# Previous value rows moved from SP's queue to ACT's in three pieces, and a deeper step pipeline in stick-breaking

## What is computed

```python
def stick_breaking(q, k, v, q_pos, k_pos):
    z = einsum('bqhd,bkhd->bhqk', q, k) * HEAD_DIM ** -0.5
    visible = k_pos[None, :] < q_pos[:, None]
    log_beta = log_sigmoid(z)
    log_keep = where(visible, log_sigmoid(-z), 0.0)
    later = cumsum(log_keep, axis=3, reverse=True) - log_keep
    w = where(visible, exp(log_beta + later), 0.0)
    return einsum('bhqk,bkhd->bqhd', w, v)
```

## Time and profile before

| | us |
|---|---|
| median of 3 runs | 1674.61 |
| lowest, highest | 1673.42, 1680.12 |
| the profiled execution, its own time | 1671.62 |
| its span, first to last instruction | 1670.0 |

### The profile page before, as it was taken

How to read it: one execution, slowest core, us unless ns; L and a number is a source line. 1 busy time by engine, 2 the same in 40 slices (tenths; PEclk the granted TensorE clock), 3 DMA queues, 4 the chain that set the end, 5 groups by cost and what they waited for, 6 DMA issues and landing times. The chain is left out here.

```text
span 1670.0 us, 31496 instructions
## 1 busy us (share of the span) xinstructions
PE 1452.1 (87%) x12700; PEld 1196.8 (72%) x12700; DVE 801.6 (48%) x1546; ACT 709.8 (43%) x1494; POOL 388.2 (23%) x364
## 2 busy tenths in 40 slices
PE   6999996800799999999999996996999999599996
PEld 6999996700688888888889883553566666477775
DVE  5656667100233433333533325774877787534341
ACT  4467776300111221122221114673556666466573
POOL 0022334100112222233223103552000000145453
PEclk9999999855899999999999997997999999799998
DMA  8554453400544323443234614123000004655651
GB/s 243 169 143 142 127 151 103 123 23 22 149 117 118 96 81 109 120 127 92 72 111 137 176 37 149 51 74 110 18 14 1 14 2 138 177 145 159 188 157 57
DMA packets 201542, 177.06 MB, mean 106 GB/s; under 512 B 30069, under 2 KB 187194, under 8 KB 201402
## 3 DMA queue, kind: packets, MB, share of 16 engines
q1 hardware_dynamic: 154921, 119.76, 24.4%
q0 software_dynamic: 28256, 46.42, 9.9%
q10 hardware_dynamic: 18224, 8.92, 1.9%
HBM read 107.60 MB, written 65.59 MB: 104 GB/s over the span
## 5 line engine op out<-in xcount | busy, mean ns | idle before, releaser
L794 PE MATMUL acc<-side_rows,side_w 128*128 128x384 f32 (+2 forms) x2448 | 454.5, 333 | 5.6 <-ACT side_stage L813 3.7
L794 PEld LDWEIGHTS acc<-side_rows,side_w 128*128 128x128 f32 x2448 | 390.6, 190 | 22.8 <-issue 7.1
L1904 DVE TENSOR_TENSOR_SCAN prod<-keepb,prod 128x512 f32<-128x512 f32 (+4 forms) x184 | 195.7, 1105 | 59.8 <-ACT keepb L1851 58.7
L813 ACT ACTIVATE side_stage<-acc 128x384 f32<-128x384 f32 (+2 forms) x102 | 46.9, 461 | 292.5 <-PE acc L794 184.3
L686 PE MATMUL acc<-side_rows,side_w 128*128 128x384 f32 (+1 forms) x864 | 150.4, 331 | 0.5 <-ACT raw L422 0.5
L686 PEld LDWEIGHTS acc<-side_rows,side_w 128*128 128x128 f32 x864 | 143.2, 189 | 2.8 <-issue 1.2
L2018 PE MATMUL b_y<-whi,mhi 128*128 128x512 f32 x272 | 110.2, 405 | 29.4 <-DVE mlo L2071 29.4
L1235 DVE COPY base<-b_two 128x256 f32<-128x256 f32 x85 | 36.1, 425 | 204.8 <-PE b_two L1036 204.8
L1851 ACT ACTIVATE keepb<-b_z 128x1024 f32<-128x1024 f32 (+4 forms) x92 | 82.0, 892 | 111.2 <-PE b_z L1771 67.4
L1047 PE MATMUL b_two<-base 64*64 64x64 f32 x1360 | 39.5, 231 | 94.0 <-ACT base L1149 93.7
L1047 PEld LDWEIGHTS b_two<-base 64*64 64x64 f32 x1360 | 28.1, 134 | 113.6 <-ACT base L1149 94.5
(11 more groups left out here) (231 smaller groups left out, 2515.6 us busy)
## 6 DMA issues: line engine op xcount, KB each, us to landing
side_rows<-hs_scratch POOLq DMA_DIRECT2D x16, 1536.0 KB, 10.3
hs_scratch<-side_rows SPq DMA_DIRECT2D x34, 512.0 KB, 4.7
mixed<-mix_scratch SPq DMA_DIRECT2D x17, 512.0 KB, 6.8
gates<-sz_scratch SPq DMA_DIRECT2D x17, 512.0 KB, 8.1
side_rows<-hs_scratch POOLq DMA_DIRECT2D x6, 1344.0 KB, 10.6
base<-in_x_prompt SPq DMA_DIRECT2D x15, 512.0 KB
xres<-in_x_prompt SPq DMA_DIRECT2D x15, 512.0 KB
out_y_prompt<-yy POOLq DMA_DIRECT2D x15, 512.0 KB, 6.5
```

Of the source, the lines that this page charges most:

```text
L794: last = pe.matmul(self.acc[:, n % 2, 0:width], w[:, w_part, k, :], rows[:, row_part, k, 0:width], start=(k == 0 and i == 0), stop=(k == K ...
L813: act.activation(self.stage[:, n % 2, 0:width], self.acc[:, n % 2, 0:width], ACT.Copy).then_inc(self.staged, 1)
L1904: dve.tensor_tensor_scan(prod[0:R, hh, c0:c0 + nk][:, ::-1], kv, kv, prod[0:R, hh, c0 + nk:c0 + nk + 1], ALU.mult, ALU.bypass).then_inc(pr ...
```

## The change

Two parts. In `delta_net` the two transfers into `vprev` leave SP's queue. They are issued by ACT, behind the loads for tile 1, and the large one is cut in two: destination partitions 1 to 112 (112 rows) and 113 to 127 (15 rows). In `stick_breaking`, `turn` runs three steps behind `scores` instead of two, `values` four instead of three, `keep_out` five instead of four, and `keepb` has three slots.

```diff
                     def _(sp):
-                        sp.dma_start(vprev[1:P, :, :], vrow[0:P - 1, :, bcols]).then_inc(prev_in, 16)
-                        sp.dma_start(vprev[0:1, 1:TILES, :], vrow[P - 1:P, 0:LAST, bcols]).then_inc(prev_in, 16)
                         side.transfers(sp, begun)
...
                                 if m == 0:
-                                    pool.wait_ge(prev_in, 32)
+                                    pool.wait_ge(prev_in, 48)
...
+                        def previous_rows():
+                            for to in (slice(1, 113), slice(113, P)):
+                                act.dma_start(vprev[to, :, :], vrow[to.start - 1:to.stop - 1, :, bcols]).then_inc(prev_in, 16)
+                            act.dma_start(vprev[0:1, 1:TILES, :], vrow[P - 1:P, 0:LAST, bcols]).then_inc(prev_in, 16)
...
                                 if m + 1 < TILES:
                                     load_tile(m + 1)
+                                if m == 0:
+                                    previous_rows()
                                 keep_beside(m, (0, 1))
...
-                keepb = sb("keepb", [P, 2, 2, KC], st=st)
+                keepb = sb("keepb", [P, 3, 2, KC], st=st)
...
-                        for s in range(N + 3):
+                        for s in range(N + 4):
...
-                            if 2 <= s < N + 2:
-                                turn(s - 2)
+                            if 3 <= s < N + 3:
+                                turn(s - 3)
...
-                            if s >= 3:
-                                values(s - 3)
+                            if s >= 4:
+                                values(s - 4)
...
-                            if s >= 2:
-                                act.wait_ge(prod_ready, 2 * (s - 1))
+                            if s >= 3:
+                                act.wait_ge(prod_ready, 2 * (s - 2))
...
-                            if s >= 2:
+                            if s >= 3:
                                 for hh in range(2):
-                                    keep_weights(act, s - 2, hh, lambda o, i: act.activation(o, i, ACT.Copy))
+                                    keep_weights(act, s - 3, hh, lambda o, i: act.activation(o, i, ACT.Copy))
...
-                            if s >= 4 and steps[s - 4][5]:
-                                dve.wait_ge(o_ready, s - 3)
-                                keep_out(rowno[s - 4])
+                            if s >= 5 and steps[s - 5][5]:
+                                dve.wait_ge(o_ready, s - 4)
+                                keep_out(rowno[s - 5])
```

More of the change, by code:

```diff
@@ L1848, in sigmoids @@
                             act.wait_ge(z_ready, s + 1)
-                            if s >= 2:
-                                act.wait_ge(prod_ready, 2 * (s - 1))
-                            act.activation(keepb[0:R, s % 2, :, 0:nk], b_z[0:R, s % 2, :, 0:nk], ACT.Sigmoid, scale=-SCALE).then_inc(keep_ready, 1)
+                            if s >= 3:
+                                act.wait_ge(prod_ready, 2 * (s - 2))
+                            act.activation(keepb[0:R, s % 3, :, 0:nk], b_z[0:R, s % 2, :, 0:nk], ACT.Sigmoid, scale=-SCALE).then_inc(keep_ready, 1)
                         def keep_keys(g):
@@ L1858, in keep_keys @@
                             act.activation(krow[:, g % 2, 0:width], b_k[:, 0:width], ACT.Copy).then_inc(krow_kept, 1)
-                        for s in range(N + 2):
+                        for s in range(N + 3):
                             if s < N:
                                 sigmoids(s)
-                            if s >= 2:
+                            if s >= 3:
                                 for hh in range(2):
-                                    keep_weights(act, s - 2, hh, lambda o, i: act.activation(o, i, ACT.Copy))
+                                    keep_weights(act, s - 3, hh, lambda o, i: act.activation(o, i, ACT.Copy))
                             if s < N:
@@ L1902, in scan @@
                             R, c0 = rows_of(m), row_base(s) + k0
-                            kv = keepb[0:R, s % 2, hh, 0:nk][:, ::-1]
+                            kv = keepb[0:R, s % 3, hh, 0:nk][:, ::-1]
                             dve.tensor_tensor_scan(prod[0:R, hh, c0:c0 + nk][:, ::-1], kv, kv, prod[0:R, hh, c0 + nk:c0 + nk + 1],
@@ L1911, in keep_out @@
                             dve.tensor_scalar(reg[:, QS + a, q0:q0 + cnt], b_o[:, 0:cnt], vend[:, a, m:m + 1], None, ALU.add).then_inc(o_kept, 1)
-                        for s in range(N + 4):
+                        for s in range(N + 5):
                             if s == 1:
```

## The result

| | us |
|---|---|
| changed kernel, median of 4 runs | 1592.55 (1585.62 to 1594.74) |
| kernel before, median of 4 runs | 1675.34 (1673.42 to 1680.12) |
| ratio | 0.9495, 95% interval 0.9459 to 0.9530 |
| profiled execution, its own time and span | 1594.74 and 1593.1 |

The kernel is 5% faster. The forecast was 1580, with a range of 1570 to 1591. The direction and the mechanism of the gain came out; the median lies 12.6 us above the forecast and 1.5 us above the range. The slices of the page answer to the earlier trace rows; one slice is now about 39.8 us.

What follows compares the result with a forecast made beforehand. PE bounds the kernel, except for a hole in delta_net behind a one-engine transfer on SP. 1671.6 - 92.9 - 1.4 + 0.5 + 1.0 = 1578.8 us, raised toward the runs' median to 1580; range 1570 to 1591.

Steps and rivals of the forecast that it cites:

- The hole: delta_net: moving the transfers off SP lets ACT find side_stage free, so PE isn't held: -92.9 us, clock -1.4 us.
- ACT pays for the issues: delta_net: three issues ahead of ACT's copies take 1.7 to 3.5 us; PE waits 0 to 0.9: +0.5 us.
- The first tile: Start of delta_net: SP's two weight loads now fall beside the first tile's loads; costed at 0, 3 us either way.
- Stick-breaking: PE's waits ahead of values move to other rows, 11.8 us against 10.3; about +1 us with one more round.
- rival B: ACT takes over a piece of SP's wait, held 5 to 12 us by the queue: 1585 to 1591; chance 0.09.
- The signs that were named: Profile after: no PE-0 slice, ACT's longest issue some 2 us, vprev landed before 335, delta_net ending some 94 us earlier.
- A: Whole kernel: the time comes out as the terms summed, 1575 to 1585 us; chance 0.80.
- C: stick_breaking: the waits at the row starts vanish, 1569 us; chance 0.04.
- D: stick_breaking: the waits multiply in rows of 2 steps, 1586 us; chance 0.03.
- E: delta_net: the large piece still runs on one engine and ACT is held instead of SP: 1668 to 1688; chance 0.03.

Runs made afterwards that it cites:

- the second bank: Against the kernel with three pieces on SP and old stick_breaking distances, values of odd rows up to 29 go to b_k: 1574.33 us, ratio 0.9385 to the kernel before.

## Why the prediction was right, and where it was off

**The hole: right.** One engine carried the 127 rows, and the queue of the issuer was held. The matmul that waited 92.9 us for ACT before waits for nothing now. The cut alone removes it (0.9462), the move alone leaves it (1.0077). By the rule of the Trainium skill, "DMA: Bandwidth & Descriptors", section "Why a DMA increments its semaphore by 16 and not by 1" (the largest number of engines up to 16 that divides the slowest dimension of both sides), 112 rows go on 16 engines, 15 rows on 15 and 127 rows on one. The trace agrees: the 2175 packets of the three pieces moved between 329 and 343 us, and the uncut transfer on ACT ran at a DMA share of 0.07. No run shows the 15 rows by themselves. The same page's section "Issuing engines are not separate DMA queues" calls the sequencer's time usually small: it was 104.9 us on ACT and 107.0 on SP for the one-engine shape, and 6.2 us for the cut one.

**ACT pays for the issues: mis-sized.** This is the term that carried most of the miss. The step was "four issues took 3.53 us together and the next 1.36", hence 1.7 to 3.5 us for three and 0.5 us on PE. They took 6.2 us, and PE lost 4.4 us: from L794's products at 327.98 to L1026 at 337.20 it took 9.2 us. Before, the same stretch ran from 322.72 to this line, 4.8 us:

```profile
327.49 0.38 PE L1028 MATMUL b_dr<-cf,base 128*128 128x128 f32 x2
```

The price had been read from a store to memory at 357 GB/s. The copy inside SBUF of about the same size took 11.0 us, and moved 235 GB/s while it had the engines to itself. The issues behind it took longer; that they waited for room behind the slower copy is the likely reason, but it was only argued. Behind the idle of 3.7 us the granted clock was 0.50 (336 to 342 us), which cost another 2.3 us (6.3 us from one L1026 to the next instead of 4.0); the sum had no term for that. The second profile of the changed kernel shows a wait of 3.4 us at the same place.

**The first tile: costed at 0, with 3 us either way.** It was +2.0 us from the stage's first matmul to L1012, within the bound. The cause is SP's transfers at the head of the stage, which in the changed kernel are the two weight loads alone, since ACT issues the pieces later: with them the wait is 5.4 us (4.8 in the second profile), with nothing there 0.9.

**Stick-breaking: right in kind.** The waits were said to move, 11.8 us against 10.3, from the 3-step rows; measured 11.4, with 4.0 where 3.1 was said for rows of 2 steps, 0.2 where 0.3 was said for rows of 3 and 3.6 where 4.1 was said for rows of 4. The reason, `keep_out` behind DVE's scans, is shown by the second bank. The stage grew by 3.1 us where 1 was forecast: 1.8 by the distances, most of the rest by the clock.

**The rest of the gap.** By the profiled executions, the span fell by 76.9 us where the terms gave 92.8. The missing 15.9 are: ACT's hold 3.9, the clock behind it 2.3, the first tile 2.0, stick-breaking 2.1; 3.5 us in the stage before, which the change doesn't touch, and 1.6 in the rest of `delta_net`; 0.5 elsewhere. The 3.5 and the 1.6 go with the clock: from 280 to 292 us it was granted at 0.83 in the changed kernel and 1.00 before (the same from 292 to 300 us), and from 513 to 517 at 0.57:

```profile
280.00:292.00 12.00, 8.53 (x62) 8.37 (x61) 8.39 (x17) 4.05 (x10) 8.28 (x10) 0.83 0.24 83
513.00:517.00 4.00, 4.00 (x40) 3.58 (x41) 0.06 (x1) 0.81 (x2) 0.00 (x0) 0.57 0.93 243
```

```profile
280.00:292.00 12.00, 8.51 (x76) 8.36 (x76) 7.91 (x16) 4.64 (x11) 8.20 (x10) 1.00 0.24 83
```

The second fence is the kernel before in the same stretch, with as much busy time but 76 products instead of 62. The second profile of the changed kernel has no loss near 513 us. Why such stretches fall where they do was not settled.

Part of this gap belongs to the two executions profiled and not to the change. In every other kept profile, also in that with the transfers left on SP (316.0), PE's first product of `delta_net` starts 1.1 to 5.9 us later than in the profile of the kernel before (310.9), which lies 3.7 us under its median, while the changed kernel's lies 2.2 us above its own. The forecast added only 1.4 us for that. The medians fall by 82.8 us. The range ended 1.5 us too low because its top, rival B, had no room for the clock behind ACT's hold.

**The signs that were named.** As said: no slice with PE 0, the L834 pair as SP's first work in the stage, waits ahead of the values of 9 to 14 us, and PE idle for less than 5 us near 327. Not as said: the wait for the first tile was over 5 us (5.4), the longest of ACT's issues took 3.7 us and not some 2, `vprev`'s packets were still moving until 343 and not 335, at less than 300 GB/s, and the first product of window attention, behind `delta_net`, came 80.7 us earlier (1014.4, now 933.8) and not some 94.

**The rivals.** What happened is B, given 0.09, and not A, given 0.80: ACT was held 6.2 us, inside B's 5 to 12, and the time lies at the top of B's 1585 to 1591. The argument against B, that a few us suffice behind a 5.5 us transfer, fell with the 5.5 us. C (the waits vanish) is refuted, of D (they multiply in rows of 2 steps) about 1 us is seen, and E holds only for the uncut transfer.

## What to carry to other kernels

Before moving a slow transfer to another queue, see how many engines carry it. Here a DMA share of 1 in 16 gave away that its shape was at fault, and cutting 127 rows into 112 and 15 cured it on either queue. Even the wide copy held its issuer for 6 us, so small pieces behind the issuer's own urgent work did better than large ones ahead of it. And where a wait stays the same when both loops are shifted by one, as here, look for another buffer and not for more distance.

## What the runs showed of the hardware

An SBUF to SBUF copy of 1 KB packets that had all engines to itself moved 235 GB/s (332.5 to 340 us of the changed kernel), a store of such packets from SBUF to memory about 357. A transfer on one engine held its queue for 105 to 107 us at the next issue, on ACT and on SP, although that was only 16 KB. And in both profiles of the changed kernel PE's wait behind ACT's issues (3.7 and 3.4 us) was followed by some us at the lower of the two clock levels (granted 0.50 from 336 to 342 us, and 0.58 from 334 to 337), so the short wait cost about half as much again.
